# The first layer's square exchanges moved from GpSimd's queue to ScalarE's, with earlier turns and smaller steps at both ends

## The chip, the cores and the metric

One core of one Trainium2 chip. The metric is the time of one execution on the device in microseconds (us), the median of several runs. The profiled rows come from one execution of the same kernel.

## What is computed

A decoder trunk of two layers over 256 positions with 2048 features, 16 heads of 128, all in float32. The part that the change touches is the first layer's mixer:

```python
def stick_breaking_layer(x, w_in, w_out):
    q, k, v, z = jnp.split(x @ w_in, 4, axis=-1)
    o = stick_breaking_attention(split_heads(q), split_heads(k), split_heads(v))
    return (merge_heads(o) * jax.nn.silu(z)) @ w_out
```

The attention takes the scores q k / sqrt(128), masks all but strictly earlier keys, and weighs the values with exp(log_sigmoid(score) + the sum of the log_sigmoid(-score) of the keys between). Each layer then adds the residual (times an alpha), normalises, and adds `(p @ w_ple) * sigmoid(x @ w_ple_gate)`. Between the layers a shared, rotary key/value projection is made of the normalised stream; the second layer uses softmax attention against it.

## The kernel before, in words

**Three products for one.** TensorE multiplies in a reduced form of float32 (fp32r). Every operand is split into a high part, which ScalarE rounds (`ACT.Copy` into an fp32r tile), and a low part, which VectorE gets as a difference. Each product is then three matmuls: high by high, high by low, low by high (L1189, L1190, L1191).

**Pieces and chunks.** A weight matrix is read in *pieces* of 256 rows by 512 columns (512 KB) and multiplied in *chunks* of 8 pieces: one chunk gives 512 output columns for all 256 positions. A piece is 12 matmuls of 512 columns. There are 392 pieces in all. SP loads piece n into one of 4 raw buffers (L326) once VectorE is done with piece n - 4. ScalarE's `split` (L480) makes the high part, once the piece has landed and TensorE has finished piece n - 8, whose buffer it takes; VectorE's `split` (L749) makes the low part. So ScalarE and VectorE may run 8 pieces ahead of TensorE.

**One order per engine, written by hand.** On ScalarE and VectorE, `pieces(n, base, after, before)` stands for the chunk that starts with piece n: for j from 0 to 7 it does the split of piece n + j + 8 and then the steps that `after` lists for j (before the split those that `before` lists). An engine's queue is in order, so a step that waits holds up all splits behind it.

**The first layer** runs over four groups of four heads. A group needs a chunk each of q, k, v and z. The order is q and k of group one, then v, z, next q, next k three times in a loop, then v and z of the last group. In chunks:

- When a q, k or z chunk is finished, VectorE turns it in squares of 32 by 32 (`turn_squares`, L770) out of the accumulator. 16 transfers (`exchange`, L430) then move the squares to their places in the transposed tile, 32 partitions by 256 numbers (32 KB) each. Before the change GpSimd issues all of them, in the order q, k, z for each group, and each exchange waits for its turn (`chunk_evac`).
- ScalarE copies the queries in `q_copies` (L503, L504; step 5 of the k chunk, step 3 in group one) and the keys in `k_copies` (L509, L510; step 4 of the v chunk). VectorE takes the low halves in `queries_lo` (L798) and `keys_lo` (L803; step 5 of the v chunk, after that step's split).
- TensorE computes the scores of two heads each after pieces 6 and 7 of the v chunk (counted from 0) in `key_scores` (L1223, L1238). They wait for the low halves.
- The rest (softplus, sums over keys, weights, values, gate) is worked off in the steps of the v, z and next q chunks.

**The start.** TensorE runs 14 warm-up matmuls (L1280) on constants. SP issues x and the weights of the first four pieces in halves, in turn (L337, L338), all from one queue; ScalarE and VectorE work on halves (L594, L597, L837, L841).

**The end.** The last gate chunk's last piece is done by token tile (`by_token`): all six matmuls of tile 0, then of tile 1. After it, `last_ple_product` does three parts: (tile 0, 512 columns), (tile 1, first 256) and (tile 1, last 256), L1357 to L1359. ScalarE takes the sigmoid of each tile (L705); VectorE multiplies (L1036) and adds (L1038) each part, and SP stores it (L378).

Of the kernel before, what the change touches and what calls it, by code (L numbers as in the profile page):

```python
# [29 lines left out]
P = 128  # L30
NEG = -1e30
LN_EPS = 1e-5
COLS = 512
PIECE_K = 2
RAWS = 4
SPLITS = 8
WARM_UPS = 14
SQUARE = 32
# [3 lines left out]
def build(nc, xt, x, pt, w_in_a, w_out_a, w_kv, w_in_b, w_out_b, w_ple, w_ple_gate,  # L42
# [6 lines left out]
    G = D // COLS  # L49
# [43 lines left out]
    with ExitStack() as ctx:  # L93
# [3 lines left out]
        def sem(name):  # L97
            return ctx.enter_context(nc.semaphore(name))
# [194 lines left out]
        x2_ready = sem("dve_x2_ready")  # L293
        q_moved = sem("dma_q_moved")
        k_moved = sem("dma_k_moved")
        z_moved = sem("dma_z_moved")
# [22 lines left out]
        def _(sp):  # L319
# [64 lines left out]
        def _(pool):  # L384
# [67 lines left out]
            for c in range(G):  # L452
                exchange(ln_turned, c + 1, gt_flat, stage[:, :], ln_moved)
                exchange(q_turned, c + 1, qT_flat, kT_flat, q_moved)
            for c in range(G):
                pool.wait_ge(sz_ready, c + G)
                exchange(chunk_evac, c + (C_Z + 1), gt_flat, vz_flat, z_moved)
            pool.wait_ge(qT_ready, 2 * G)
# [15 lines left out]
        def _(act):  # L474
# [19 lines left out]

            def copy_qT(k, dst):

                act.wait_ge(q_moved, k * MOVED + MOVED)
                nc.scalar.activation(by_square(dst), qT_x, ACT.Copy, scale=SCALE).then_inc(qT_ready, 1)
# [57 lines left out]

            def silu_z(k, dst):
                act.wait_ge(z_moved, k * MOVED + MOVED)
                nc.scalar.activation(by_square(dst), gt_x, ACT.Silu).then_inc(sz_ready, 1)
# [27 lines left out]


            for j in range(RAWS):
                for i, (x_sem, w_sem, x_done, w_done) in enumerate((  # L590
# [127 lines left out]
            with act.Fori(1, G) as c:  # L718
                pieces(c * PC + N_Q, N_Q, {2: [lambda: ln_hi(c - 1)], 3: [lambda: normalise_x2(c)],
                                           6: [lambda: copy_qT(c + (G - 1), quarter(q_all, c - 1))]})  # L720
            pieces(N_Z, N_Z, {2: [lambda: ln_hi(G - 1)], 6: [lambda: copy_qT(2 * G - 1, quarter(q_all, G - 1))]})
            act.wait_ge(x2_spilled, 16 * G)
            with act.Fori(1, G) as c:
                pieces(c * PC + N_Z, N_Z, {5: [lambda: silu_z(c + (G - 1), quarter(sz_all, c - 1))]})
            act.wait_ge(act_ready, S_KV + G)
            pieces(N_KV, N_KV, {5: [lambda: silu_z(2 * G - 1, quarter(sz_all, G - 1)), lambda: queries_hi_b(G)]})

# [17 lines left out]
        def _(dve):  # L745
# [138 lines left out]
            pieces(n, 0, v_steps(G - 1, n))  # L884
            pieces(n + PC, 0, z_steps(G - 1, n + PC))

# [199 lines left out]
            def z_end(c, parity):  # L1086
                def earlier_moved():
                    dve.wait_ge(z_moved, c * MOVED + (G * MOVED))
                return {PC - 1: [earlier_moved, lambda: turn_squares(c * PC + (N_Z + PC), parity, vz_flat)]}
# [4 lines left out]
            with dve.Fori(1, G) as c:  # L1094
                pieces(c * PC + N_Q, N_Q, {2: [lambda: ln_quarter(c - 1)], 3: [lambda: ln_lo(c - 1), lambda: normalise_x2(c)],
                                           4: [lambda: turn_normed(c)],
                                           6: [lambda: dve.wait_ge(q_moved, c * MOVED + (G * MOVED))]} | q_end(c, c % 2))
            pieces(N_Z, N_Z, {2: [lambda: ln_quarter(G - 1)], 3: [lambda: ln_lo(G - 1)]} | z_end(0, 0))
# [74 lines left out]
        def _(pe):  # L1173
            def piece(n, r, operand, tiles, out_banks, first, final, by_token=False, halves=False):

# [6 lines left out]
                for i, t in sorted(order, key=lambda it: it[1]) if by_token else order:  # L1182
# [13 lines left out]
            def chunk(n, base, operand, parity, c, quarters=None, after=None, last=False):  # L1196

                if not isinstance(c, int) or c >= 2:
                    pe.wait_ge(chunk_evac, c - 1)
                for j in range(PC):  # L1200
# [4 lines left out]
                    elif quarters is not None and j % 2 == 0:  # L1205
                        pe.wait_ge(act_ready, quarters + j // 2 + 1)
                    piece(n + j, (base + j) % SPLITS, operand, range(PIECE_K * j, PIECE_K * (j + 1)),
                          acc_of(parity), j == 0, j == PC - 1, by_token=last and j == PC - 1, halves=halves)
                    for step in (after or {}).get(j, ()):
# [103 lines left out]
            def ple_and_gate(layer):  # L1313
# [34 lines left out]
            def last_ple_product():  # L1348
# [4 lines left out]
                for bank, (t, lo, hi) in enumerate(LAST_PARTS):  # L1353
                    for i in range(PIECE_K):
# [102 lines left out]
```

## Time and profile before

| | us |
|---|---|
| median of 3 runs (lowest, highest) | 1149.44 (1148.65, 1149.66) |
| the profiled execution's own time | 1152.77 |
| its span, first to last instruction | 1151.1 |

| engine | busy us | share of the span |
|---|---|---|
| TensorE, matmuls | 1139.9 | 99% |
| TensorE, weight loads | 951.0 | 83% |
| VectorE | 745.8 | 65% |
| ScalarE | 590.9 | 51% |
| GpSimd | 232.6 | 20% |

The times in the rows below count from the start of the span. PE is TensorE, DVE VectorE, ACT ScalarE, POOL GpSimd, SPq the queue of SyncE that issues loads. Matmuls are pipelined: a record of a 512-column matmul is 0.39 us long, but the next begins 0.227 us after it, so a busy TensorE is read by the steps between starts. An arrow `<-` in brackets names what ended the idle time before an instruction. The mean granted clock of TensorE over the span was 0.999 of full speed.

### The profile page before, as it was taken

To read this page: it belongs to the slowest core of one execution; us is meant where nothing else is said; L and a number is where in the kernel's file an instruction comes from. 1 tells how busy PE (TensorE), PEld (TensorE's weight loads), DVE (VectorE), ACT (ScalarE), POOL (GpSimd) and SP (SyncE) were. 2 spreads that over 40 slices of the span, in tenths; PEclk is the share of its full clock that TensorE was granted. 3 is DMA by queue.
4 is the path that set the end of the run, shared out by engine and by line. 5 is a ranking of instruction groups with operands and counts; after the bars stand their busy time and mean duration, and the time that the engine had idled before them with its cause. 6 is when DMAs were issued, how large, how long until landed. Compare 5 with 4: busy or idle time off the path is not lost.

```text
span 1151.1 us, 15530 instructions
## 1 busy us (share of the span) xinstructions
PE 1139.9 (99%) x5274; PEld 951.0 (83%) x5274; DVE 745.8 (65%) x795; ACT 590.9 (51%) x669; POOL 232.6 (20%) x475
## 2 busy tenths in 40 slices
PE   9989999999999999999999999999999999999998
PEld 8878888888888888888888888888888888888887
DVE  6646556556465657578888785456776676656873
ACT  6555557446556453546454555555554545334641
POOL 1222320340232300002536753420000010000000
PEclk9999999999999999999999999999999999999999
DMA  9866775675676686457787876774555575763571
GB/s 305 270 208 178 208 217 151 195 228 171 185 209 178 199 311 217 148 164 256 228 275 228 246 243 215 226 218 149 183 161 183 159 243 162 258 199 117 190 239 70
DMA packets 126587, 235.67 MB, mean 205 GB/s; under 512 B 13856, under 2 KB 16160, under 8 KB 126032
## 3 DMA queue, kind: packets, MB, share of 16 engines
q1 hardware_dynamic: 110176, 209.74, 59.0%
q0 software_dynamic: 16368, 25.37, 6.8%
q8 instruction: 24, 0.39, 0.1%
q14 instruction: 19, 0.16, 0.0%
HBM read 216.71 MB, written 4.19 MB: 192 GB/s over the span
## 4 chain that ended last, share of the span: by engine, by line
PE 91%; DMA 3%; DVE 1%; POOL 1%; ACT 1%; issue 1%; SPq 1%; DVEq 0%; ACTq 0%
PE acc L1189 28%; PE acc L1191 28%; PE acc L1190 28%; DMA raw<-in_w_in_a 3%; PE aux L1223 2%; POOL heads L430 1%; PE aux L1216 1%; ACT w_hi L480 1%; DMA heads<-big 1%; PE aux L1249 1%; PE aux L1263 1%; DVE w_lo L749 1%; PE aux L1394 0%; PE aux L1238 0%; PE aux L1191 0%
## 5 line engine op out<-in xcount | busy, mean ns | idle before, releaser
L749 DVE TENSOR_TENSOR w_lo<-raw,w_hi 128x1024 fp32r<-128x1024 f32 x388 | 470.1, 1222 | 344.9 <-ACT w_hi L480 344.6
L480 ACT ACTIVATE w_hi<-raw 128x1024 fp32r<-128x1024 f32 x388 | 408.9, 1058 | 441.7 <-PE acc L1191 360.3
L1189 PE MATMUL acc<-w_hi,act 128*128 128x512 f32 x1548 | 608.0, 393 | 0.1
L1191 PE MATMUL acc<-w_hi,act 128*128 128x512 f32 x1548 | 603.1, 390 | 0.0
L1190 PE MATMUL acc<-w_lo,act 128*128 128x512 f32 x1548 | 602.6, 389 | 0.0
L1191 PEld LDWEIGHTS acc<-w_hi,act 128*128 128x128 f32 x1548 | 290.7, 188 | 61.4
L1189 PEld LDWEIGHTS acc<-w_hi,act 128*128 128x128 f32 x1548 | 290.9, 188 | 59.4 <-issue 0.7
L1190 PEld LDWEIGHTS acc<-w_lo,act 128*128 128x128 f32 x1548 | 291.0, 188 | 58.8
L430 POOL DMA_DIRECT2D heads<-big x192 | 93.8, 497 | 281.9 <-DVE big L770 238.1
L430 POOL DMA_DIRECT2D heads<-v_or_z x64 | 31.2, 496 | 52.0 <-DVE v_or_z L770 39.1
L430 POOL DMA_DIRECT2D stage<-v_or_z x48 | 23.5, 499 | 69.5 <-DVE v_or_z L988 43.7
L430 POOL DMA_DIRECT2D heads<-stage x64 | 31.4, 498 | 18.5 <-DVE stage L1077 16.9
L430 POOL DMA_DIRECT2D heads<-heads x64 | 32.0, 509 | 8.6 <-DVE heads L1065 8.4
L415 POOL TENSOR_TENSOR rstd<-var_eps,minus_half 128x2 f32<-128x2 f32 x3 | 2.1, 716 | 142.2 <-DVE var_eps L925 142.2
L493 ACT ACTIVATE act<-stage 128x1024 fp32r<-128x1024 f32 (+1 forms) x12 | 12.7, 1061 | 32.4 <-DVE stage L945 32.4
L461 POOL COPY heads<-big 128x512 f32 x4 | 2.5, 616 | 128.9 <-PE aux L1223 128.9
L576 ACT ACTIVATE heads<-aux,neg_max 128x128 f32<-128x128 f32 (+1 forms) x32 | 13.0, 420 | 23.6 <-DVE neg_max L1112 23.6
L764 DVE TENSOR_TENSOR act<-stage,act 128x1024 fp32r<-128x1024 f32 (+1 forms) x12 | 14.7, 1224 | 9.0 <-ACT act L493 9.0
L945 DVE TENSOR_SCALAR stage<-aux,ln_col 128x256 f32<-128x256 f32 x32 | 15.2, 536 | 0.9 <-PE aux L1216 0.9
L1223 PE MATMUL aux<-q_parts,k_parts 128*128 128x256 f32 x48 | 9.9, 321 | 5.6 <-DVE k_parts L803 5.6
L770 DVE STREAM_TRANSPOSE big<-acc 128x1024 f32<-128x1024 f32 x12 | 14.9, 1243 | 0.0
L493 ACT ACTIVATE act<-heads 128x1024 f32 (+1 forms) x8 | 8.5, 1062 | 11.7 <-DVE heads L826 11.7
(158 smaller groups left out, 653.2 us busy)
## 6 DMA issues: line engine op xcount, KB each, us to landing
raw<-in_w_in_a SPq DMA_DIRECT2D x124, 512.0 KB, 3.9
raw<-in_w_ple_gate SPq DMA_DIRECT2D x64, 512.0 KB, 4.8
raw<-in_w_in_b SPq DMA_DIRECT2D x64, 512.0 KB, 4.6
raw<-in_w_kv SPq DMA_DIRECT2D x64, 512.0 KB, 3.9
raw<-in_w_out_a SPq DMA_DIRECT2D x32, 512.0 KB, 4.5
raw<-in_w_out_b SPq DMA_DIRECT2D x32, 512.0 KB, 4.8
heads<-big POOLq DMA_DIRECT2D x192, 32.0 KB, 3.4
heads<-in_ln_rows POOLq DMA_DIRECT2D x4, 1024.0 KB, 7.9
```

Of the source, the lines that this page charges most:

```text
L430: pool.dma_start(dst[g * SQUARE:(g + 1) * SQUARE, a * HT // NS:(a + 1) * HT // NS], src[a * SQUARE:(a + 1) * SQUARE, g * HT // NS:(g + 1) ...
L480: nc.scalar.activation(w_hi[:, r], raw[:, r % RAWS], ACT.Copy).then_inc(hi_ready, 1)
L493: nc.scalar.activation(quarter(dst[:, 0], c), src, ACT.Copy).then_inc(act_hi, 1)
L576: last = nc.scalar.activation(prob[:, b, h, lo:hi], aux_b[:, 2 * b + h, lo:hi], ACT.Exp, bias=neg_max[:, b, i:i + 1], accum_out=row_sum[:, ...
L749: nc.vector.tensor_tensor(w_lo[:, r], raw[:, r % RAWS], w_hi[:, r].bitcast(F32), ALU.subtract) \
L764: nc.vector.tensor_tensor(quarter(dst[:, 1], c), src, quarter(dst[:, 0], c).bitcast(F32), ALU.subtract).then_inc(act_ready, 1)
L770: nc.vector.transpose(turned_squares(dst), turned_rows(acc_of(parity))).then_inc(chunk_evac, 1)
L945: last = nc.vector.tensor_scalar(dst, part, g, b, ALU.mult, ALU.add)
L1189: nc.tensor.matmul(dst, hi, w_hi[:, r, i], start=begin, stop=False)
L1190: nc.tensor.matmul(dst, hi, w_lo[:, r, i], start=False, stop=False)
L1191: mm = nc.tensor.matmul(dst, lo, w_hi[:, r, i], start=False, stop=end)
L1223: mm = nc.tensor.matmul(dst, lhs(a), rhs(b), start=start and i == 0, stop=True, skip_group_check=True)
```

## The change

Five things are changed together.

1. Two warm-up matmuls fewer (12).
2. The two weight halves of the first piece are issued by ScalarE, ahead of its first instruction, and no longer by SP.
3. All twelve exchanges of the first layer are issued by ScalarE, right after the first split (j = 0) of the chunk that follows the turned one. The second layer's exchanges stay with GpSimd and count on semaphores of their own (`q_moved_b`, `z_moved_b`).
4. The first two turns come earlier in VectorE's order: the queries' after step 2 (was 3), the keys' after step 3 (was 6). `keys_lo` stands before the split of step 5, not behind it.
5. The first part of the last PLE product is done between tile 0 and tile 1 of the last gate piece.

```diff
-WARM_UPS = 14
+WARM_UPS = 12
...
@@ sync
                     sp.dma_start(x_raw[:, PIECE_K * j + i], xt[rows, :]).then_inc(x_sem, 16)
-                    sp.dma_start(raw[:, j, i], wa[rows, 0:COLS]).then_inc(w_sem, 16)
+                    if j > 0:
+                        sp.dma_start(raw[:, j, i], wa[rows, 0:COLS]).then_inc(w_sem, 16)
@@ gpsimd
-            for g in range(G):
-                exchange(chunk_evac, g * 4 + 1, qT_flat, qn, q_moved)
-                exchange(chunk_evac, g * 4 + 2, kT_flat, kn, k_moved)
-                exchange(chunk_evac, g * 4 + 4, gt_flat, zn, z_moved)
@@ scalar
+            for i, w_sem in enumerate((w_half_landed[0], w_landed[0])):
+                act.dma_start(raw[:, 0, i], w_in_a[0][i * P:(i + 1) * P, 0:COLS]).then_inc(w_sem, 16)
...
+            def exchange(turned, count, dst, src, moved):
+
+                act.wait_ge(turned, count)
+                for a in range(NS):
+                    for g in range(NS):
+                        act.dma_start(dst[g * SQUARE:(g + 1) * SQUARE, a * HT // NS:(a + 1) * HT // NS],
+                                      src[a * SQUARE:(a + 1) * SQUARE, g * HT // NS:(g + 1) * HT // NS]) \
+                            .then_inc(moved, 16)
+
+            def move_k(k):
+                exchange(chunk_evac, k * 4 + 2, kT_flat, kn, k_moved)
+
+            def move_q(k):
+                exchange(chunk_evac, k * 4 + 1, qT_flat, qn, q_moved)
+
+            def move_z(k):
+                exchange(chunk_evac, k * 4 + 4, gt_flat, zn, z_moved)
+
             def after_k(k):
-                return {5: [lambda: q_copies(k)]}
+                return {0: [lambda: move_q(k)], 5: [lambda: q_copies(k)]}
 
             def after_v(k):
-                return {4: [lambda: k_copies(k)], 6: [lambda: exp_abs(k, 0)],
+                return {0: [lambda: move_k(k)], 4: [lambda: k_copies(k)], 6: [lambda: exp_abs(k, 0)],
                         7: [lambda: values_hi(k), lambda: exp_abs(k, 1), lambda: log_1p(k)]}
...
             def gate_group(k):
-                return {5: [lambda: silu_z_group(k)], 6: [lambda: gated_hi(k, k)]}
+                return {0: [lambda: move_z(k)], 5: [lambda: silu_z_group(k)], 6: [lambda: gated_hi(k, k)]}
 
             pieces(0, 0)
-            pieces(PC, 0, {3: [lambda: q_copies(0)]})
+            pieces(PC, 0, {0: [lambda: move_q(0)], 3: [lambda: q_copies(0)]})
@@ vector
             def v_steps(k, n):
-                return {5: [lambda: keys_lo(k)],
-                        7: [lambda: values_lo(k), lambda: evacuate_v(n, 0, vn_a), lambda: softplus(k, 0)]}
+                return {7: [lambda: values_lo(k), lambda: evacuate_v(n, 0, vn_a), lambda: softplus(k, 0)]}
...
-            pieces(0, 0, {3: [lambda: turn_squares(PC, 0, qn)]})
-            pieces(PC, 0, {4: [lambda: queries_lo(0)], 6: [lambda: turn_squares(2 * PC, 1, kn)]})
+            pieces(0, 0, {2: [lambda: turn_squares(PC, 0, qn)]})
+            pieces(PC, 0, {3: [lambda: turn_squares(2 * PC, 1, kn)], 4: [lambda: queries_lo(0)]})
             with dve.Fori(0, G - 1) as g:
                 n = g * (4 * PC) + 2 * PC
-                pieces(n, 0, v_steps(g, n))
+                pieces(n, 0, v_steps(g, n), before={5: [lambda: keys_lo(g)]})
@@ tensor
                     if by_token and t == 0 and end:
                         mm.then_inc(tile_0_done, 1)
+                        if between:
+                            between()
...
-                    chunk(c * PC + n, n, act0, c % 2, c + c0, last=True)
-                    last_ple_product()
+                    chunk(c * PC + n, n, act0, c % 2, c + c0,
+                          last=lambda: last_ple_product(LAST_PARTS[0:1]))
+                    last_ple_product(LAST_PARTS[1:])
```

## Rows read from the trace of the kernel before

**Rows 1.** The page, part 1: busy us, share of the span, instructions.

```profile
PE 1139.9 (99%) x5274; PEld 951.0 (83%) x5274; DVE 745.8 (65%) x795; ACT 590.9 (51%) x669; POOL 232.6 (20%) x475
```

**Rows 2.** Waits of TensorE: us in total, times, longest.

```profile
PE aux L1223 <- DVE k_parts L803: 5.6, 4, 4.4
```

**Rows 3.** TensorE's timeline (start, us) at scores of groups one, two; clock window.

```profile
73.91 0.98 PE L1223 MATMUL aux<-q_parts,k_parts 128*128 128x256 f32 x3 [4.37 <-DVE k_parts L803]
79.25 0.52 PE L1223 MATMUL aux<-q_parts,k_parts 128*128 128x256 f32 x3
170.14 0.59 PE L1223 MATMUL aux<-q_parts,k_parts 128*128 128x256 f32 x3 [0.38 <-DVE k_parts L803]
174.12 0.52 PE L1223 MATMUL aux<-q_parts,k_parts 128*128 128x256 f32 x3
core 0: us, PE busy (x) PEld busy (x) DVE busy (x) ACT busy (x) POOL busy (x), PEclk, DMA share, GB/s
...
74.00:75.00 1.00, 1.00 (x6) 1.00 (x6) 0.90 (x1) 0.00 (x0) 0.00 (x0) 0.50 0.53 74
```

**Rows 4.** The start: last warm-ups by source line; timeline of ScalarE and TensorE.

```profile
L1280 PE MATMUL aux<-stage x7: 275/275/275, 5.6 to 6.3; 128*128 128x128 f32 x7
...
2.96 0.42 ACT L594 ACTIVATE act<-big 128x256 fp32r<-128x256 f32 x1 [0.86 <-DMA big<-in_xt]
...
6.57 0.63 ACT L597 ACTIVATE w_hi<-raw 128x512 fp32r<-128x512 f32 x1 [1.48 <-DMA raw<-in_w_in_a]
...
8.07 0.47 PE L1189 MATMUL acc<-w_hi,act 128*128 128x512 f32 x1
```

**Rows 5.** SP's issues by source line: duration ns lowest/median/highest, first and last start.

```profile
L338 SPq DMA_DIRECT2D raw<-in_w_in_a x8: 421/432/599, 1.3 to 8.1; - x8
...
L326 SPq DMA_DIRECT2D raw<-in_w_in_a x122: 367/373/686, 12.3 to 353.8; - x122
...
L378 SPq DMA_DIRECT2D out<-big x3: 340/368/368, 1147.2 to 1148.7; - x3
```

**Rows 6.** GpSimd's timeline, one exchange of 16 transfers (group two's keys).

```profile
154.58 7.81 POOL L430 DMA_DIRECT2D heads<-big  x16 [13.18 <-DVE big L770]
```

**Rows 7.** ScalarE's timeline in the first group.

```profile
39.38 1.06 ACT L480 ACTIVATE w_hi<-raw 128x1024 fp32r<-128x1024 f32 x1 [1.86 <-DMA raw<-in_w_in_a]
...
50.18 3.06 ACT L480 ACTIVATE w_hi<-raw 128x1024 fp32r<-128x1024 f32 x3
...
56.41 1.28 ACT L480 ACT_TABLE_LOAD   x1 [1.01 <-DMA raw<-in_w_in_a]
...
69.81 0.63 ACT L509 ACTIVATE big<-heads 128x512 f32<-128x512 f32 x1 [3.59 <-DMA heads<-big]
70.35 0.61 ACT L510 ACTIVATE k_parts<-heads 128x512 fp32r<-128x512 f32 x1
```

**Rows 8.** DMA issues of the whole span: count, KB each, median us to landing.

```profile
raw<-in_w_in_a SPq DMA_DIRECT2D x124, 512.0 KB, 3.9
...
heads<-big POOLq DMA_DIRECT2D x192, 32.0 KB, 3.4
```

**Rows 9.** VectorE's timeline in the first group.

```profile
33.74 3.45 DVE L749 TENSOR_TENSOR w_lo<-raw,w_hi 128x1024 fp32r<-128x1024 f32 x3
...
55.80 1.25 DVE L770 STREAM_TRANSPOSE big<-acc 128x1024 f32<-128x1024 f32 x1
...
73.08 0.68 DVE L803 TENSOR_TENSOR k_parts<-heads,k_parts 128x512 fp32r<-128x512 f32 x1
```

**Rows 10.** Group two: VectorE's turn of the keys; ScalarE's first copy of them.

```profile
153.05 1.24 DVE L770 STREAM_TRANSPOSE big<-acc 128x1024 f32<-128x1024 f32 x1
...
165.83 0.63 ACT L509 ACTIVATE big<-heads 128x512 f32<-128x512 f32 x1 [0.42 <-DMA heads<-big]
```

**Rows 11.** The end: timeline of VectorE, with TensorE's last matmul.

```profile
1145.72 0.69 DVE L1036 TENSOR_TENSOR stage<-aux,stage 128x512 f32<-128x512 f32 x1 [14.92 <-PE aux L1359]
...
1146.73 0.28 PE L1359 MATMUL aux<-w_hi,act 128*128 128x256 f32 x1
...
1147.84 0.41 DVE L1036 TENSOR_TENSOR stage<-aux,stage 128x256 f32<-128x256 f32 x1
1148.29 0.42 DVE L1038 TENSOR_TENSOR big<-big,stage 128x256 f32<-128x256 f32 x1
```

More of the change, by code:

```diff
@@ L294, in build @@
         q_moved = sem("dma_q_moved")
+        q_moved_b = sem("dma_q_moved_b")
+        z_moved_b = sem("dma_z_moved_b")
         k_moved = sem("dma_k_moved")
@@ L453, in _ @@
                 exchange(ln_turned, c + 1, gt_flat, stage[:, :], ln_moved)
-                exchange(q_turned, c + 1, qT_flat, kT_flat, q_moved)
+                exchange(q_turned, c + 1, qT_flat, kT_flat, q_moved_b)
             for c in range(G):
                 pool.wait_ge(sz_ready, c + G)
-                exchange(chunk_evac, c + (C_Z + 1), gt_flat, vz_flat, z_moved)
+                exchange(chunk_evac, c + (C_Z + 1), gt_flat, vz_flat, z_moved_b)
             pool.wait_ge(qT_ready, 2 * G)
@@ L493, in operand_hi, with copy_qT @@
                 nc.scalar.activation(quarter(dst[:, 0], c), src, ACT.Copy).then_inc(act_hi, 1)
-            def copy_qT(k, dst):
-                act.wait_ge(q_moved, k * MOVED + MOVED)
+            def copy_qT(c, dst):
+                act.wait_ge(q_moved_b, c * MOVED + MOVED)
                 nc.scalar.activation(by_square(dst), qT_x, ACT.Copy, scale=SCALE).then_inc(qT_ready, 1)
@@ L555, in stick_weights, with silu_z @@
                 nc.scalar.activation(prob[:, b], scores_of(b), ACT.Exp).then_inc(w_ready, 1)
-            def silu_z(k, dst):
+            def silu_z(k, dst, z_moved=z_moved):
                 act.wait_ge(z_moved, k * MOVED + MOVED)
@@ L719, in _ @@
                 pieces(c * PC + N_Q, N_Q, {2: [lambda: ln_hi(c - 1)], 3: [lambda: normalise_x2(c)],
-                                           6: [lambda: copy_qT(c + (G - 1), quarter(q_all, c - 1))]})
-            pieces(N_Z, N_Z, {2: [lambda: ln_hi(G - 1)], 6: [lambda: copy_qT(2 * G - 1, quarter(q_all, G - 1))]})
+                                           6: [lambda: copy_qT(c - 1, quarter(q_all, c - 1))]})
+            pieces(N_Z, N_Z, {2: [lambda: ln_hi(G - 1)], 6: [lambda: copy_qT(G - 1, quarter(q_all, G - 1))]})
             act.wait_ge(x2_spilled, 16 * G)
             with act.Fori(1, G) as c:
-                pieces(c * PC + N_Z, N_Z, {5: [lambda: silu_z(c + (G - 1), quarter(sz_all, c - 1))]})
+                pieces(c * PC + N_Z, N_Z, {5: [lambda: silu_z(c - 1, quarter(sz_all, c - 1), z_moved_b)]})
             act.wait_ge(act_ready, S_KV + G)
-            pieces(N_KV, N_KV, {5: [lambda: silu_z(2 * G - 1, quarter(sz_all, G - 1)), lambda: queries_hi_b(G)]})
+            pieces(N_KV, N_KV, {5: [lambda: silu_z(G - 1, quarter(sz_all, G - 1), z_moved_b), lambda: queries_hi_b(G)]})
             def after_v_b(k, n):
@@ L883, in _ @@
             n = N_OUT[0] - 2 * PC
-            pieces(n, 0, v_steps(G - 1, n))
+            pieces(n, 0, v_steps(G - 1, n), before={5: [lambda: keys_lo(G - 1)]})
             pieces(n + PC, 0, z_steps(G - 1, n + PC))
@@ L1087, in earlier_moved @@
                 def earlier_moved():
-                    dve.wait_ge(z_moved, c * MOVED + (G * MOVED))
+                    if c > 0:
+                        dve.wait_ge(z_moved_b, c * MOVED)
                 return {PC - 1: [earlier_moved, lambda: turn_squares(c * PC + (N_Z + PC), parity, vz_flat)]}
@@ L1096, in _ @@
                                            4: [lambda: turn_normed(c)],
-                                           6: [lambda: dve.wait_ge(q_moved, c * MOVED + (G * MOVED))]} | q_end(c, c % 2))
+                                           6: [lambda: dve.wait_ge(q_moved_b, c * MOVED)]} | q_end(c, c % 2))
             pieces(N_Z, N_Z, {2: [lambda: ln_quarter(G - 1)], 3: [lambda: ln_lo(G - 1)]} | z_end(0, 0))
@@ L1173, in _, with piece @@
         def _(pe):
-            def piece(n, r, operand, tiles, out_banks, first, final, by_token=False, halves=False):
+            def piece(n, r, operand, tiles, out_banks, first, final, by_token=False, halves=False, between=None):
                 if halves:
@@ L1193, in piece, with chunk @@
                         mm.then_inc(tile_0_done, 1)
+                        if between:
+                            between()
                 mm.then_inc(piece_used, 1)
-            def chunk(n, base, operand, parity, c, quarters=None, after=None, last=False):
+            def chunk(n, base, operand, parity, c, quarters=None, after=None, last=None):
                 if not isinstance(c, int) or c >= 2:
@@ L1207, in chunk @@
                     piece(n + j, (base + j) % SPLITS, operand, range(PIECE_K * j, PIECE_K * (j + 1)),
-                          acc_of(parity), j == 0, j == PC - 1, by_token=last and j == PC - 1, halves=halves)
+                          acc_of(parity), j == 0, j == PC - 1, by_token=last and j == PC - 1, halves=halves, between=last)
                     for step in (after or {}).get(j, ()):
@@ L1352, in last_ple_product @@
                 pe.wait_ge(p_kept, 1)
-                for bank, (t, lo, hi) in enumerate(LAST_PARTS):
+                for t, lo, hi in parts:
+                    bank = LAST_PARTS.index((t, lo, hi))
                     for i in range(PIECE_K):
```

2 lines of the change are left out of this document (1 added, 1 removed).

## The prediction

> **What bounds the kernel now.** I began with the page's busy times. TensorE is busy for 1139.9 of the span's 1151.1 us [rows 1], and ScalarE and VectorE for 51 and 65%. Nothing that makes a free engine faster helps; only the places where TensorE stands still count. There are few. The waits of TensorE name one reason outside the start: the low half of the keys (VectorE, L803), four times, 5.6 us together, 4.4 of them in the first head group [rows 2]. Then I read TensorE's timeline at both kinds of place [rows 3]. In the first group the scores begin at 73.91 after 4.37 us of idle time. TensorE had started its last matmul 0.39 us before that, so it could have gone on at about 69.4. That is 4.5 us lost. And the idle time costs a second time: the granted clock is 0.50 from 74 to 75 us, that is 1.2 GHz in place of 2.4, right after the engine stood still. From the first to the second pair of scores it takes 79.25 - 73.91 = 5.34 us there, and 174.12 - 170.14 = 3.98 us in the next group, where the clock stayed up: 1.36 us more. In groups two to four it is the rest of the 5.6, 1.2 us of idle time (0.38 in group two), and with the 0.16 us by which a matmul's record outlasts its step about 0.55 us each. In all, the keys cost 4.5 + 1.4 + 1.6 = 7.5 us.
>
> Pace, used below: from 8.07 [rows 4] to 69.4 TensorE does 270 matmuls of 512 columns, 0.227 us each, a piece of 12 in 2.725 us and a chunk of 8 pieces in 21.8. So chunk one (queries) ends at 28.5, chunk two (keys) at 50.3, and the scores are wanted 7 pieces later.
>
> **The start.** Two warm-ups fewer are four records fewer; the last ones have a step of 0.112 us [rows 4], so the first real matmul can come 4 x 0.112 = 0.45 us sooner. The next six wait for the second half of the first weights: ScalarE idled 1.48 us for them until 6.57, and TensorE took them up at 8.07, about 0.28 us late. SP had issued them fourth, each issue costing 0.43 us [rows 5]; ScalarE now issues them second, some 0.9 us sooner, and SP's eight loads behind them move up by two issues. The same bytes must still come through the same 16 engines, so I count less than the 0.9: between 0 and 0.8 us, and take 0.3. ScalarE's two issues (0.9 us) let its table load end at about 3.0 us, and the first x is taken up at 2.96 [rows 4]: nothing.
>
> **The moves on ScalarE.** This is the largest part. Twelve exchanges of 16 transfers each leave GpSimd, where one exchange takes 7.81 us (0.49 a transfer) [rows 6] and delays nobody, since GpSimd has no other work there. They go into ScalarE's queue behind the first split of a chunk. Behind them stand the splits of the next pieces, then the copies. No row shows a transfer issued by ScalarE. The nearest are SP's: 0.373 us inside a loop, 0.432 outside [rows 5], for 512 KB as for 256, so the price looks fixed; on SP one follows another with some 0.04 us between. I take a step of 0.43 us, 6.9 us per exchange, and keep 0.37 and GpSimd's 0.49 as ends. In total ScalarE gets 192 x 0.43 = 83 us more work in the first 400 us.
>
> *First group.* ScalarE's split 16 ends at about 40.0 (it starts at 39.38 now [rows 7]; fewer transfers compete for the memory there). The queries have been turned long before: VectorE now does it after split 10, waits at most 0.3 us for TensorE's 28.5, and behind it stands split 11, whose weights land at 30.3 only. Their exchange issues until 46.9. Splits 17 to 19 follow at 1.02 us each (3.06 for three [rows 7]) to 50.0. The queries land 3.4 us after their last issue at 46.5 [rows 8], at 49.9, just in time: copies until 52.0. VectorE ends split 19 at 51.5 and turns the keys until 52.7, which is 4.3 us sooner than now (55.80 + 1.25 [rows 9]). But the raw buffers are four: the load of piece 24 waits until VectorE has done piece 20 (54.2), and takes 3.9 us [rows 8] and a little for the loads ahead: 58.3. The table load that stands before split 24 (1.28) and the split (1.06) bring it to 60.6; now it is about 58.8. Only then come the keys' 16 transfers: until 67.5. Splits 25 to 28 until 71.6, the two key copies (about 1.15 us with the overlap, [rows 7]) until 72.8. VectorE ends split 28 at 73.2 (1.15 us a split [rows 9]) and the keys' low half, which no longer has split 29 ahead of it, 0.68 later: 73.9. The scores start at 74.0, against 73.91 now. What the earlier turn and the new place of the low half win, two bursts in ScalarE's queue take away. With the 0.3 us of the start: -0.2 us. The clock falls again. Each 0.01 us of the issue step moves this by 32 x 0.01 = 0.32 us: with 0.37 it is -2.1, with 0.49 +1.7.
>
> The landing time: the Trainium skill ("DMA: Bandwidth & Descriptors", Latency and other measured facts) gives about 0.6 us to the first byte for a transfer of SP or ScalarE and about 1 us for one of GpSimd. By that the queries would land 0.4 us sooner, but ScalarE is busy with splits until 50.0, so the sum would stay within 0.1 us of mine; no row here shows it for ScalarE.
>
> *Groups two to four.* Here ScalarE is well ahead. Count from a chunk's end (in group two 170.14 - 0.55 - 7 x 2.725 = 150.5). The turn of the squares ends at +3.8 [rows 10]. ScalarE issues from +3.9 to +10.8, and does four splits until +15.0. The load of the sixth piece waits for VectorE at +13.0 and lands at +16.9; split, query copies and two more splits take ScalarE to +22.9, and VectorE turns the keys 4.0 us after the next chunk's end, 0.2 later than now. So the delay hardly adds up. In the V chunk: issues until +11.0, four splits until +15.1, copies until +16.3, VectorE's fourth split until +16.8, low half +17.5. Wanted at 7 x 2.725 = +19.1. Now GpSimd ends its issues at 162.4 and the copies start at 165.83, +15.3, so the low half is late only because split 29 is ahead of it. The 0.55 us go three times: -1.6 us, with 1.6 us to spare. The z squares move in the same way, and their copy at +16.9 waits for no transfer: 0. GpSimd's next work, the load of the residual, waits for the last values as before, and the new semaphores of the second layer count the same events: 0.
>
> **The end.** The last PLE product's first part goes between the two token tiles of the last gate piece. TensorE's work is the same and still ends at 1146.73 + 0.28. But VectorE today starts its six steps at 1145.72 and runs them without a break to 1148.71 [rows 11]; the last product would be free to start at 1147.1 and starts at 1147.84. Moved up by six matmuls, the first product and sum (2 x 0.7) are over at about 1145.8. The sigmoid of the second tile comes later by the same six matmuls, 1.36 us, ending at about 1146.25; the next product starts at 1146.35, its sum at 1146.80, the last product at 1147.15 and the last sum at 1147.6, 0.7 us sooner than 1148.29: -0.7 us, between -0.3 and -0.8.
>
> **Sum:** -0.2 - 1.6 - 0.7 = -2.5 us. The profiled execution took 1152.77 us, 1.67 outside its span; the median of the three runs is 1149.44, 3.3 less than the profiled one, and I apply the difference to that: 1146.9. About 0.2% (2.3 us) is what a measurement can tell from no change, so this stands close to that line.
>
> **Rivals.**
> *A transfer costs ScalarE much less than SP.* Below a step of 0.28 us the first scores are ready before 69.4 (74.0 less 4.9 us, over 32 issues). Then the whole 7.5 us go, with the start and the end: -7.5 - 0.5 - 0.7 = -8.7, 1140.7. Against it: no row of SP is under 0.34. For it: these transfers carry 32 rows, not 128 or 256. Chance 0.14.
> *ScalarE becomes the bound* (slower). Place: splits 25 to 28 behind the keys' exchange. It decides from about 0.48 us a transfer, where the 1.6 us to spare in groups two to four are used up (32 issues between the queries' and the keys' burst). At 0.55: the first scores +3.8 - 0.3, groups two to four 3.8 - 1.6 - 0.55 = +1.7 each, the end -0.7: +7.9, 1157.3; at 0.50 it is about +1.3, 1150.7. For it: SP's startup issues beside a busy queue reach 0.60 us [rows 5]. Against it: the typical ones. Chance of over 0.2% slower 0.27.
> The Trainium skill speaks on this side too: "Perfetto Trace Analysis" (DMA Instruction, HWDGE) says that two sequencers share one descriptor generator under a lock; two or three of the 16 issues would then wait one SP issue, about 1 us more per burst, an estimate from SP's 0.37 us. No run here shows it. The result would be that of a step of 0.49.
> *The later waits stay*, if a split is late in a way that I don't see: -0.2 - 0.7 = -0.9, 1148.5. Chance 0.12.
> The forecast with its ends at 0.37 and 0.47 us (1145 to 1148.5) has 0.47; a little over half of it is over 0.2% faster.
>
> **Numbers.** Faster 0.14 + 0.28 = 0.42; within 0.2% 0.19 + 0.12 = 0.31; slower 0.27. The range goes from the cheap transfer to a step of about 0.52: 1141 to 1154.
>
> **What would show it.** Rows of ScalarE's transfers with a step of 0.41 to 0.45 us, 16 in a row; the first wait of the scores still about 4.5 us and the clock at 0.50 after it; none in groups two to four; the keys' turn at 51.5 instead of 55.80; VectorE's last steps with gaps and the last sum 0.7 us nearer to TensorE's end. A first wait under 2 us, or waits over 1 us in later groups, would prove my issue price wrong; waits before weight pieces (L1189) would prove the buffer argument wrong.

## The result, and the profile after

The changed kernel takes 1182.52 us in the median of four runs (1180.67 to 1184.03), against 1149.38 (1148.65 to 1149.66) for the kernel before: 1.0288 times as long, with a 95% interval of 1.0271 to 1.0304. So it is 33 us slower, outside the range, where 2.5 us less were forecast. Its profiled execution took 1180.67 us with a span of 1179.0, which is 27.9 us more than the span before; the traces are compared span against span.

The page of the kernel after, parts 1 to 4 and 6 (the columns as in [rows 1]; part 4 is the chain that ended last; part 6 gives count, KB and us to landing):

```profile
PE 1146.9 (97%) x5270; PEld 957.4 (81%) x5270; DVE 742.2 (63%) x795; ACT 585.7 (50%) x669; POOL 139.0 (12%) x283
...
PEclk9989998998999899999999999999999999999999
...
PE 86%; ACTq 5%; DVE 3%; issue 2%; ACT 2%; DMA 1%; DVEq 0%; POOL 0%; SPq 0%; POOLq 0%
...
heads<-big ACTq DMA_DIRECT2D x192, 32.0 KB, 2.3
```

TensorE is busy 7.0 us longer with the same matmuls (four warm-up records fewer), and the row of granted clock shows why: four dips in the first 14 of its 40 slices. ScalarE's *busy* time even fell, by 5 us, though it has 192 transfers more to issue: a look at busy times alone shows nothing. The chain has them, as "ACTq", with 5% of the span. TensorE's waits, and its timeline at the scores of groups one and three:

```profile
PE aux L1244 <- DVE k_parts L822: 27.3, 4, 7.3
```

```profile
75.37 0.98 PE L1244 MATMUL aux<-q_parts,k_parts 128*128 128x256 f32 x3 [6.24 <-DVE k_parts L822]
...
82.05 0.51 PE L1244 MATMUL aux<-q_parts,k_parts 128*128 128x256 f32 x3
...
283.02 0.98 PE L1244 MATMUL aux<-q_parts,k_parts 128*128 128x256 f32 x3 [6.96 <-DVE k_parts L822]
...
288.38 0.52 PE L1244 MATMUL aux<-q_parts,k_parts 128*128 128x256 f32 x3
```

The same stretch as one row of the view by windows (columns as in [rows 3]):

```profile
75.00:80.00 5.00, 4.63 (x16) 4.18 (x17) 2.67 (x3) 3.76 (x4) 0.00 (x0) 0.50 0.98 321
```

The one reason of before [rows 2] is there again, four times, and now each wait is long: 27.3 us in place of 5.6. After each, the clock is down: from the first to the second pair of scores it takes 82.05 - 75.37 = 6.68, 5.73, 288.38 - 283.02 = 5.36 and 6.83 us, where an undisturbed group takes 3.98 [rows 3]. Added up over the four groups that is 8.7 us more, against 1.36 before. With the start (-0.4: TensorE could have gone on at 68.97 and not at 69.38) and the end (-0.64) the account is 21.7 + 7.3 - 0.4 - 0.6 = +28.0, and 27.9 are measured. All of the loss is in the four waits for the keys' low half and in the slow clock behind them.

Why they are long stands in ScalarE's timeline of group two (a row with x16 holds 16 transfers in a row):

```profile
111.14 10.16 ACTq L615 DMA_DIRECT2D heads<-big  x16
...
137.71 10.16 ACTq L615 DMA_DIRECT2D heads<-big  x16
148.05 3.90 ACT L479 ACTIVATE w_hi<-raw 128x1024 fp32r<-128x1024 f32 x4 [12.27 <-PE acc L1210]
154.38 1.06 ACT L479 ACTIVATE w_hi<-raw 128x1024 fp32r<-128x1024 f32 x1 [2.43 <-DMA raw<-in_w_in_a]
...
163.00 10.18 ACTq L615 DMA_DIRECT2D heads<-big  x16
173.38 3.89 ACT L479 ACTIVATE w_hi<-raw 128x1024 fp32r<-128x1024 f32 x4 [11.77 <-PE acc L1210]
177.18 0.61 ACT L508 ACTIVATE big<-heads 128x512 f32<-128x512 f32 x1
```

and VectorE's of the same group:

```profile
161.73 1.24 DVE L789 STREAM_TRANSPOSE big<-acc 128x1024 f32<-128x1024 f32 x1
162.89 1.18 DVE L768 TENSOR_TENSOR w_lo<-raw,w_hi 128x1024 fp32r<-128x1024 f32 x1
174.46 4.63 DVE L768 TENSOR_TENSOR w_lo<-raw,w_hi 128x1024 fp32r<-128x1024 f32 x4 [10.39 <-ACT w_hi L479]
179.01 0.68 DVE L822 TENSOR_TENSOR k_parts<-heads,k_parts 128x512 fp32r<-128x512 f32 x1
```

A burst of 16 takes 10.16 us, a step of (10.16 - 0.61) / 15 = 0.64 us with a single transfer's 0.61, where the sum had 0.43. The copies at 177.18 come without a pause behind four splits that were held up by the burst; they waited for no landing. And the bursts add up. Chunk three of this group (V) begins when the scores are wanted less 7 pieces, at 172.13 + 0.23 - 19.07 = 153.3, the keys' chunk 21.8 us sooner. Counted from its own chunk's end, the queries' squares are turned at 137.68 - 131.5 = +6.2 and the keys' at 162.97 - 153.3 = +9.7; forecast were +3.8 and +4.0. The burst for z of the group before, at 111.14, makes the queries' turn late, their burst makes the keys' turn later still, and then the third burst stands ahead of the copies. The low half ends at +26.4, with +19.1 wanted and +17.5 forecast: 5.7 us of the delay are the later turn and 3.3 the longer last burst.

### The profile page after: what moved, and what is told of

Read it like the earlier page. It is cut to its first block, busy times and chain, and to the rows that moved or that the text cites. A ratio compares the mean times of both kernels' runs of the same rounds, so it can differ in the third digit from the quotient of the medians.

```text
span 1179.0 us, 15531 instructions
## 1 busy us (share of the span) xinstructions
PE 1146.9 (97%) x5270; PEld 957.4 (81%) x5270; DVE 742.2 (63%) x795; ACT 585.7 (50%) x669; POOL 139.0 (12%) x283
## 3 DMA queue, kind: packets, MB, share of 16 engines
q0 software_dynamic: 10224, 19.07, 5.0%
q10 hardware_dynamic: 9504, 6.83, 2.1%
## 4 chain that ended last, share of the span: by engine, by line
PE 86%; ACTq 5%; DVE 3%; issue 2%; ACT 2%; DMA 1%; DVEq 0%; POOL 0%; SPq 0%; POOLq 0%
PE acc L1208 27%; PE acc L1210 26%; PE acc L1209 26%; ACTq L615 5%; PE aux L1244 2%; DVE w_lo L768 2%; DMA raw<-in_w_in_a 1%; ACT w_hi L479 1%; PE aux L1237 1%; PE aux L1270 1%; PE aux L1284 1%; DVE big L789 1%; PE aux L1417 0%; PE aux L1259 0%; PE aux L1301 0%
## 5 line engine op out<-in xcount | busy, mean ns | idle before, releaser
L479 ACT ACTIVATE w_hi<-raw 128x1024 fp32r<-128x1024 f32 x388 | 404.5, 1057 | 483.6 <-PE acc L1210 345.3
L403 POOL DMA_DIRECT2D big<-in_x x4 | 2.9, 722 | 401.1 <-PE aux L1284 401.1
L1244 PE MATMUL aux<-q_parts,k_parts 128*128 128x256 f32 x48 | 12.3, 379 | 27.3 <-DVE k_parts L822 27.3
L1244 PEld LDWEIGHTS aux<-q_parts,k_parts 128*128 128x128 f32 x48 | 9.5, 257 | 29.2 <-issue 28.8
```

The lines of the kernel that those rows point to most:

```text
L479: nc.scalar.activation(w_hi[:, r], raw[:, r % RAWS], ACT.Copy).then_inc(hi_ready, 1)
L1244: mm = nc.tensor.matmul(dst, lhs(a), rhs(b), start=start and i == 0, stop=True, skip_group_check=True)
```

## The experiments

**Price of a transfer.** Theory A1, as it was on record: the price hangs on the shape, 32 rows from SBUF to SBUF are dear on either queue, and 128 rows cost 0.43. Rivals: it is dear because ScalarE issues it (A2), or only beside SP's issues (A3). The groups also vary the memory at either end, and whether the data crosses partitions. The kernel computes no layer (its outputs are zeros) and issues groups of eight transfers, each group when the one before has landed:

```diff
+for i in range(8):   # the third group, 32x64; others: 32x256, 128x256, 16x256, from HBM, to HBM, same rows, by SP
+    act.dma_start(two[32:64, i * 64:(i + 1) * 64], one[0:32, i * 64:(i + 1) * 64]).then_inc(a_done, 16)
```

> The disputed price by itself: no layer is computed, zeros are stored; ScalarE and then SP issue groups of eight transfers of one shape. Theory A1 (the price hangs on the shape: 32 rows between SBUF and SBUF are dear on either queue): about 0.61 us on ScalarE and on SP alike for 32x256, and 0.43 for 128 rows. Rival A2 (ScalarE is dearer than SP): 0.61 on ScalarE for every shape, 0.37 to 0.43 on SP. Rival A3 (only beside SP's loads is it dear, by a shared generator): 0.43 for all with the other queue at rest, more only in the last group, where both issue at once.

Its timeline. In order, ScalarE: 32 x 256, 128 x 256, 32 x 64, 16 x 256; HBM to SBUF 32 x 256 and 128 x 512; SBUF to HBM; 32 x 256 within the same partitions; 64 x 256. Then SP: 32 x 256, 128 x 256, HBM to SBUF. The last two rows are both engines at once:

```profile
13.70 5.05 ACTq L43 DMA_DIRECT2D two<-one  x8
20.02 5.09 ACTq L46 DMA_DIRECT2D two<-one  x8
26.59 5.05 ACTq L49 DMA_DIRECT2D two<-one  x8
32.78 5.00 ACTq L52 DMA_DIRECT2D two<-one  x8
39.00 3.70 ACTq L55 DMA_DIRECT2D two<-in_w_in_a  x8
44.10 3.74 ACTq L58 DMA_DIRECT2D two<-in_w_in_a  x8
53.33 3.64 ACTq L61 DMA_DIRECT2D spill<-two  x8
58.15 5.00 ACTq L64 DMA_DIRECT2D two<-one  x8
64.42 5.24 ACTq L67 DMA_DIRECT2D two<-one  x8
71.24 5.00 SPq L78 DMA_DIRECT2D three<-one  x8
77.49 5.02 SPq L81 DMA_DIRECT2D three<-one  x8
83.99 3.64 SPq L84 DMA_DIRECT2D three<-in_w_in_a  x8
88.96 5.01 SPq L87 DMA_DIRECT2D three<-one  x8
89.02 5.28 ACTq L71 DMA_DIRECT2D two<-one  x8
```

With the other queue at rest, eight transfers within SBUF take 5.00 to 5.24 us (0.63 to 0.66 each) and eight with one end in HBM 3.6 to 3.7 (0.46), whatever the rows, the bytes, the partitions or the issuing engine. So A2 and A3 fall, and A1 was right on the engine and wrong on the rows: 128 rows within SBUF cost 0.64 and not 0.43. What decides is whether one end is in HBM. SP's rows [rows 5] were the wrong kind of transfer, not the wrong engine. Why a transfer within SBUF is dearer to issue no run here shows.

**Which part does it.** Everything but item 3, and item 3 alone. The edit is the first kernel's (the keys' move goes back in the same way); the second is the kernel before with ScalarE's exchanges and nothing else:

```diff
-                return {0: [lambda: move_q(k)], 5: [lambda: q_copies(k)]}
+                return {5: [lambda: q_copies(k)]}
+            for g in range(G):   # back in GpSimd's queue: queries, keys, z
+                exchange(chunk_evac, g * 4 + 1, qT_flat, qn, q_moved)
```

> The changed kernel with the first layer's exchanges back in GpSimd's queue; everything else of the change stays. Theory A (the loss is ScalarE's issue time, 10.2 us per exchange in front of the splits and the key copies): the waits of the scores go in all four groups, since the keys are turned 4 us earlier in group one and their low half has no split ahead of it; against the kernel before that is 7.5 us of waits and slow clock, 0.4 at the start and 0.6 at the end less: 1141 us. Rival B (one of the other parts, the earlier turns, the low half ahead of the split or the smaller start, holds VectorE up): a good part of the 33 us stays, above 1160 us. Rival C (the exchanges contend with the weights for the DMA engines wherever they are issued): the first wait stays near 4.4 us, 1147 us.

> The kernel before with nothing but the exchanges moved to ScalarE's queue. Theory A: all of the loss is here, and a little more, since the keys are turned late and their low half stands behind a split of 1.2 us in each group: four waits of 8 to 12 us, 1184 to 1195 us. Rival B (the loss comes from the other parts): within 3 us of 1149.

With GpSimd's exchanges the rest of the change takes 1144.18 us (1143.18 to 1144.62), 0.9951 times the time of before (0.9936 to 0.9966): 5.0 us faster, and 38.3 less than the whole change. The scores wait no more, and TensorE's list of waits is down to the warm-ups' wait at the very start, which the kernel before has too:

```profile
PE aux L1305 <- POOL stage L390: 1.4, 1, 1.4
```

The expectation of 1141 had subtracted 8.5 us, and by just that much its span is shorter than that of before (1151.1 - 1142.6). But before's profiled execution, 1152.77, was 3.3 us above the median of its own kernel, and only 5 us stand between the medians: waits read from one execution had been taken off the median of others. Item 3 alone gives 1194.54 (1193.19 to 1195.12), ratio 1.0387 (1.0369 to 1.0406), with the first wait at 12.4 and the others at 9.3 to 9.9:

```profile
PE aux L1242 <- DVE k_parts L819: 41.3, 4, 12.4
```

So the moves cost 38 us beside the other items and 45 without them.

**Fewer transfers.** If the price per issue decides, half as many transfers of twice the size must free the kernel. In these two the squares keep their own rows, so the transposition across rows is left out (by the run above the price of an issue is the same within and across partitions); all else is computed.

```diff
-                for a in range(NS):
+                for a in range(2):                                   # 8 transfers of 64 KB
+                for lo, hi in ((0, 384), (384, 768), (768, 1024)):   # 12, in the other kernel
```

> The changed kernel with 8 transfers of 64 KB per exchange in place of 16 of 32 KB, the same bytes; each square keeps its rows, so the transposition across rows is left out. Theory A (time in ScalarE's queue is transfers times 0.64 us): bursts of 5.1 us, below the 7.7 at which the waits of groups two to four begin; these are gone, the first is 1 to 2 us, and the time 1141 to 1144. Rival C (bytes, contention, landing): as the changed kernel, over 1170.

> As the run with 8 transfers, with 12 (384, 384 and 256 columns); each square keeps its rows, so the transposition across rows is left out. Theory A: bursts of 7.7 us, just where the waits of groups two to four begin by the step forecast in the prediction (0.48 x 16 = 7.7): 0 to 0.7 us there; the first wait 1.35 us plus 4 transfers, 3.9 us, with the slow clock after it. 1148 to 1152. If the prediction's margin was wrong the waits of groups two to four are 2 us and more, over 1155.

The bursts of the two, from ScalarE's timelines:

```profile
149.87 5.04 ACTq L616 DMA_DIRECT2D heads<-big  x8
```

```profile
153.81 7.61 ACTq L616 DMA_DIRECT2D heads<-big  x12
```

and the waits of the kernel with twelve:

```profile
PE aux L1245 <- DVE k_parts L823: 4.0, 4, 2.5
```

Eight transfers: 1146.39 us, 2.4 above the upper end of what was expected; of the scores only the first wait (1.35 us). Twelve: 1151.54, the first wait 2.5 where 3.9 was expected, the others 0.49, 0.33 and 0.62. Each is one run beside a median of 1149.22 and 1149.47 for before. The burst of 7.61 us is just past the point where groups two to four begin to be late; the prediction's margin had put that point at 16 x 0.48 = 7.7 us. The first scores come at 70.8, 71.8 and 75.4 for 8, 12 and 16. From 8 to 16 that is 4.6 us for a burst longer by 5.1: about one burst stands in their way, not two. The steps are uneven, 1.0 us for the first four transfers more and 3.6 for the last four; why was not followed up.

**Which exchange.** Theory: what ScalarE's keys cost is their burst, and what the queries' and z's cost is the late turn. Rival: each exchange costs the same wherever it stands.

```diff
+            for g in range(G):   # keys on ScalarE: these two back to GpSimd
+                exchange(chunk_evac, g * 4 + 1, qT_flat, qn, q_moved)
+                exchange(chunk_evac, g * 4 + 4, gt_flat, zn, z_moved)
...
+            for g in range(G):   # the other kernel: only the keys back to GpSimd
+                exchange(chunk_evac, g * 4 + 2, kT_flat, kn, k_moved)
```

> The changed kernel with the queries' and z's exchanges back in GpSimd's queue; only the keys' stay with ScalarE. Theory A (a burst of 10.3 us stands before the four splits and the key copies, and bursts in successive chunks add up through VectorE and the raw buffers): from a chunk's end, keys turned at +3.8, issues until +14.2, copies until +19.2, low half +20.6, wanted at +19.1: waits of 1.7 us in groups two to four; in group one, where one burst counts, still 5 to 6 us and the slow clock. Against e1 +14 us, 1158. Rival D (the loss is the same for each exchange moved, 38 us over 12): a third of it, 13 us in all, but spread evenly, 3 us in each group.

> The opposite: queries and z on ScalarE, the keys on GpSimd. Theory A: the queries' burst makes VectorE turn the keys at +9.7 from the chunk's end, as in the changed kernel; GpSimd issues until +17.8, landing +21.2, copies +22.3, low half +23: waits of about 4 us in groups two to four; nothing in group one, where the landing at 65 is early enough. 1144 + 13 = 1157 us. Rival D (the same for each exchange): 25 us, 1169. Rival E (only the keys' own burst matters): 1144.

Waits of the first kernel, then of the second:

```profile
PE aux L1247 <- DVE k_parts L825: 9.2, 4, 4.5
```

```profile
PE aux L1246 <- DVE k_parts L824: 15.4, 4, 5.3
PE aux L1239 <- DVE big L1004: 1.8, 1, 1.8
...
PE acc L1210 <- DVE big L912: 1.3, 1, 1.3
```

Keys alone: 1158.0 us (1155.97 to 1159.3), ratio 1.0073 (1.0052 to 1.0094), as the theory had it; the rival's total was within 1 us of that. But the rival wanted some 3 us in each group, and the waits are 4.5, 1.4, 1.4 and 2.0 us, with 2.3 us of slow clock behind the first and 1.6 behind the last. Queries and z: 1169.57 (1167.38 to 1171.21), ratio 1.0174 (1.0152 to 1.0196). The late turn is there, before any burst of the keys:

```profile
154.28 1.24 DVE L791 STREAM_TRANSPOSE big<-acc 128x1024 f32<-128x1024 f32 x1
```

It ends 9.3 us behind its chunk's end at 146.2. The waits of the scores are 1.1 us in group one, where the theory had none, and 4.6, 5.3 and 4.4 in the others, where it had about 4. The total is 12 us above its 1157 and agrees with the rival's 1169. The theory's total had left out 3.4 us of these waits, two other waits (3.1 us) and the slow clock behind the three long ones (5.9 us). Both totals fit the rival as well; the uneven waits and the place of the turn speak for the theory. Against the 1144.2 of the kernel without moves the two cost 14 and 25 us, 39 together, and all three exchanges 38: they add.

**The same transfers, spread.** Four behind each of the splits 0 to 3, so no split waits for more than four (but for the first queries, whose last eight stand behind split 2).

```diff
-                return {0: [lambda: move_k(k)], 4: [lambda: k_copies(k)], 6: [lambda: exp_abs(k, 0)],
+                return spread(move_k, k) | {4: [lambda: k_copies(k)], 6: [lambda: exp_abs(k, 0)],
+            def spread(move, k):
+                return {j: [lambda j=j: move(k, j)] for j in range(NS)}
```

> The changed kernel with each exchange's 16 transfers spread on ScalarE, four behind each of the splits 0 to 3 of the chunk. ScalarE issues the same 192 transfers, but VectorE gets its splits and SP its free buffers sooner. Theory A with adding up through the buffers: the keys are turned at about +5 instead of +9.7, copies until +20.7, low half +21.4: waits of 2.4 us instead of 7.2 in groups two to four, the first unchanged near 6: 1182 - 20 = 1162. Rival F (the total of ScalarE's time before the key copies counts, wherever it stands): 1180 to 1184, as the changed kernel.

ScalarE's timeline, the queries of group two:

```profile
136.38 1.06 ACT L479 ACTIVATE w_hi<-raw 128x1024 fp32r<-128x1024 f32 x1 [3.12 <-issue]
136.40 2.46 ACTq L616 DMA_DIRECT2D heads<-big  x4
139.04 1.06 ACT L479 ACTIVATE w_hi<-raw 128x1024 fp32r<-128x1024 f32 x1 [1.59 <-issue]
139.05 2.46 ACTq L616 DMA_DIRECT2D heads<-big  x4
```

1154.59 us (1153.09 to 1155.06), ratio 1.0042 (1.0027 to 1.0056): the same 192 transfers, 28 us less than in bursts, and 7 less than expected. The rows say why: the four issues begin 0.02 us after the split and run beside it. Four of them and a split take 139.04 - 136.38 = 2.66 us, not 2.57 + 1.06. The later scores wait no more, where 2.4 us each were expected; 4.94 us at the first ones and a wait of 2.1 at 436 us stay, and it is still 10.4 us behind GpSimd's exchanges. At the first scores the copies of the keys now wait for the last transfer to land, and no longer for splits:

```profile
72.09 0.63 ACT L508 ACTIVATE big<-heads 128x512 f32<-128x512 f32 x1 [1.61 <-DMA heads<-big]
```

**The gain of the rest.** Item 4 alone, and the warm-ups of the fastest kernel put back to 14:

```diff
-            pieces(0, 0, {3: [lambda: turn_squares(PC, 0, qn)]})
-            pieces(PC, 0, {4: [lambda: queries_lo(0)], 6: [lambda: turn_squares(2 * PC, 1, kn)]})
+            pieces(0, 0, {2: [lambda: turn_squares(PC, 0, qn)]})
+            pieces(PC, 0, {3: [lambda: turn_squares(2 * PC, 1, kn)], 4: [lambda: queries_lo(0)]})
...
-WARM_UPS = 12
+WARM_UPS = 14
```

> The kernel before with the fourth part of the change alone: the two earlier turns and the keys' low half ahead of the split; the exchanges stay with GpSimd. If the waits of the scores are what e1 wins, they are gone here too, and the time is e1's without 0.4 us at the start and 0.6 at the end: 1145.2 us. If start and end bring most of it, it stays within 1 us of the kernel before, 1148 to 1150.

> The run with GpSimd's exchanges, with 14 warm-ups in place of 12. In the changed kernel the first real matmul came at 6.29 us, no sooner than 6.32 before, since the clock rose at 6.1 instead of 5.2 us. If the clock's rise shifts by itself, not by the warm-ups, the first real matmul comes 4 x 0.112 to 4 x 0.213 us later, at 6.7 to 7.1, and takes up the second half late: +0.3 to 0.6 us at most. If two more warm-ups bring the rise back to 5.2, it starts at 6.3 and nothing changes: 1144.2.

Item 4 alone takes 1145.12 us (1144.84 to 1145.52), ratio 0.9961 (0.9948 to 0.9974): 4.0 of the 5.0 us, and no wait of the scores. Of the other 1.0 the end gives 0.64 in the traces; for the start they show no gain, as the next section tells. With 14 warm-ups the other takes 1144.32 (1143.62 to 1149.35) against 1144.18 with 12: no difference, as the second of the two expectations had it. Their warm-up records, by source line in the window from 3 to 7.2 us (duration in ns lowest, median, highest), with 12 and with 14:

```profile
L1305 PE MATMUL aux<-stage x19: 421/421/421, 2.6 to 6.4; 128*128 128x128 f32 x19
```

```profile
L1305 PE MATMUL aux<-stage x23: 275/275/422, 2.6 to 5.9; 128*128 128x128 f32 x23
```

## Why the prediction was wrong

- **Issue price (the step that failed):** "the price looks fixed", a step of 0.43 us with ends at 0.37 and 0.49. It was 0.64, above both ends. That SP's price did not change with the size was right and led nowhere: it is fixed for each kind, and every row of [rows 5] has one end in HBM, while an exchange has both in SBUF. GpSimd's 0.49 [rows 6] was the only row of the right kind, and GpSimd issues the same exchange for less than ScalarE (0.49 against 0.64). With no row of that kind on SP's or ScalarE's queue, the upper bound could not be closed at 0.49.
- **The rival "ScalarE becomes the bound"** is what happened. Its place (splits behind the keys' exchange) and, within half a microsecond or so, its point (0.48 us, a burst of 7.7) are shown by the twelve transfers. Its price, 1157.3 at 0.55, stretched to 0.64 by its own slopes is 32 x 0.21 = 6.7 us at every place: 6.4 at the first scores, 6.7 - 1.6 - 0.55 = 4.6 at each of the three others, -0.7 at the end, +19.4 in all, where the spans differ by 27.9. (By the same slopes its +1.3 at 0.50 should have been some 1.5.) The rest: the first scores came only 1.5 us later (-4.9); the other waits grew by 19.8 us and not 13.7 (+6.1), since three bursts push on one another, which the prediction had denied ("the delay hardly adds up"); and the clock behind the four waits cost 7.3 us that the rival had at nothing. The medians differ by 33.1 and not 27.9 because before's profiled execution was 3.4 us above its median and this one's 1.9 below.
- **First scores:** forecast 74.0, measured 75.37 with the dear issue; the slope of 32 issues was wrong. The queries' burst was forecast from 40.0 to 46.9; it began at 36.66, since split 16 came sooner and the issues ran beside it, and ended at 47.30. So its higher price was nearly all absorbed, and the table load that precedes split 24 came at 58.38 against a forecast of 58.3 for its weights. The keys' burst too ran beside the instructions ahead of it, the table load and split 24, and so began at 58.52 and not at 60.6:

```profile
58.52 1.20 ACTq L615 DMA_DIRECT2D heads<-big  x2
59.67 1.06 ACT L479 ACTIVATE w_hi<-raw 128x1024 fp32r<-128x1024 f32 x1
59.75 8.95 ACTq L615 DMA_DIRECT2D heads<-big  x14
```

With 32 x 0.21 us more the scores would have come at about 80.7; with 3.3 for the keys' burst alone, less these 2.1, it is 75.2. That issues run beside a running instruction was nowhere in the sum, and here it hid a part of the dear price.
- **The turn in group one and the buffer argument:** right. The keys' turn was forecast for 51.5 and came at 51.92, and there was no wait ahead of weight pieces.
- **Groups two to four:** with twelve transfers the margin of 1.6 us would have left about 0.1 to spare, and 0.3 to 0.6 us of wait were measured: it was about half a microsecond too large. Eight transfers left these groups without a wait; the sign was wrong for the price of an issue and for what it sets off. The win of 0.55 us each by the earlier low half is there once the bursts are gone.
- **The start:** the second weight half is taken up at 7.77 in place of 8.07, the 0.3 that was taken. That was luck. The two kernels with the old start (item 3 alone and item 4 alone) take it up at 7.71 and 7.69, so 8.07 need not be the old start's usual time, and the new start with GpSimd's exchanges has 8.18. The 0.45 of two warm-ups is not there: the first real matmul starts at 6.29 against 6.32, because more of the warm-ups took 421 ns and not 275.
- **The size of the win:** "the keys cost 4.5 + 1.4 + 1.6 = 7.5 us" was read rightly from an execution 3.3 us above its kernel's median. Removing these waits gives 4.0 us between medians (item 4 alone), so only about half of the 7.5 shows in the usual execution. Applying the difference to the median, as the sum did, doesn't mend that.
- **The end:** VectorE ends 1176.19 + 0.42 - (1175.27 + 0.28) = 1.06 us behind TensorE, against 1.70 [rows 11]: 0.64 less where 0.7 was forecast, with the gap that was named:

```profile
1173.63 0.69 DVE L1056 TENSOR_TENSOR big<-big,stage 128x512 f32<-128x512 f32 x1
1174.94 0.42 DVE L1054 TENSOR_TENSOR stage<-aux,stage 128x256 f32<-128x256 f32 x1 [0.63 <-PE aux L1382]
...
1176.19 0.42 DVE L1056 TENSOR_TENSOR big<-big,stage 128x256 f32<-128x256 f32 x1
```

- **Landing:** the Trainium skill's "DMA: Bandwidth & Descriptors" (Latency and other measured facts), with 0.6 and 1 us to the first byte, made it 0.4 us sooner from ScalarE. It was 1.1 us sooner (2.3 against 3.4), in the same direction, and as forecast it changed nothing: the copies stood behind splits.
- **The shared lock:** the Trainium skill's "Perfetto Trace Analysis" (DMA Instruction, HWDGE) was read as about 1 us more per burst. With SP and ScalarE issuing at once, eight transfers took 5.28 and 5.01 us against 5.05 and 5.00 alone, at most 0.03 us a transfer. No run here shows the wait of 1 us.
- **The size of it all:** the Trainium skill's "DMA: Bandwidth & Descriptors" (Issuing engines are not separate DMA queues) calls the sequencer's time for initiating a DMA "usually small relative to the DMA itself". Here one issue takes 0.64 us and its transfer lands after 2.3 us, so a single issue is the smaller part; but sixteen in a row hold ScalarE for 10.2 us, which is not small, and that is what counted.

## What to carry to other kernels

Price a transfer by its kind: look for a row that has both its ends in the same memories, and where there is none, leave the upper bound open or say what would happen at twice the price. A run of transfers in an engine's in-order queue is one long instruction to all that stands behind it (10.2 us here), and its delay can come back in the next chunk, as it did here through VectorE's later turn; spread it between compute steps, or leave it with an engine that is idle, even if that one lands each transfer later. Busy shares do not show it; count the idle time that it gives the bound engine, and add the slow clock behind each long wait. Compare the profiled execution's time with its kernel's median before a wait read from it is counted as a win.

## What the runs showed that was not expected

- Issuing a transfer within SBUF costs ScalarE and SP 0.63 us each and one with an end in HBM 0.46, from 8 to 128 KB and 16 to 128 rows (256 KB with an end in HBM). GpSimd issues the exchange of 32 KB transfers in 0.49 each.
- ScalarE issues transfers while its previous ACTIVATE still runs (136.38 and 136.40), and beside a table load (58.38 and 58.52); but the next ACTIVATE waits for the last issue.
- Behind a wait of the scores of 2.0 us (keys alone, group four) to 12.4 us (item 3 alone) the clock is at 0.50 for a time, and that costs 1.3 to 2.9 us more; behind waits of up to 1.4 us nothing is lost. Waits of about equal length differ: 6.24 and 6.96 us were followed by 2.7 and 1.4 us lost. In part the slow stretch had begun inside the wait, where it costs nothing: the mean clock in the first three waits of the changed kernel is 0.92, 0.79 and 0.72, with 2.7, 1.8 and 1.4 us lost behind them. The fourth, 0.70 and 2.9 us, does not fit, so what sets the difference stays open.
- The warm-ups' records fall from 421 to 275 ns at 4.4 to 5.2 us in the four traces with 14 warm-ups, and at 6.1 us or later in the seven with 12. This reads like the clock's rise, though the column of the granted clock has 1.00 from 4 us on in all of them. The number can hardly act by itself, since with 14 the fall comes before the added ones run; and it changes nothing in the end, 1144.18 against 1144.32 us. What sets the moment, and whether it differs from execution to execution of one kernel, was not tried.
